# Dealing the sixteen row slots of a two-table expert gather from one pool instead of eight per table

## The chip, the cores and the metric

One Trainium2 chip, one core. The metric is the device time of one execution of the program, in microseconds (us). Names of the engines: PE is TensorE, DVE is VectorE, ACT is ScalarE, POOL is GpSimd, SP is SyncE.

## What is computed

A decoder trunk of two layers over 256 tokens of 1024 float32 features. Layer 0 is a short gated convolution and an expert network, layer 1 stick-breaking attention and an expert network of the same form; a final norm ends it. The expert network is what matters here:

```python
def one_chunk(xc):                                   # 128 tokens
    q = (xc @ w_query).reshape(C, HEADS, 2, KEY_DIM) # 8 heads
    ...
    idx = ...                                        # 16 experts of 16384 per token and head
    gate = softmax(top_s)
    act = gelu(einsum('chkd,cd->chk', u_tbl[idx], xc))
    coef = gate * act
    return einsum('chk,chkd->cd', coef, v_tbl[idx])
```

For each token, head and choice one row of 1024 floats is read from the table u and one from the table v. That is 2 layers x 2 chunks x 8 heads x 16 choices = 512 gathers from u and 512 from v; one gather fetches a row for each of 128 tokens, 512 KB.

## The kernel before, in words

The work on the experts runs in 32 steps (`STEPS`, one chunk and head each, number n), and a step has two groups g of eight choices. The text numbers the groups K = 2n + g, from 0 to 63, and calls the sixteen gathers of a group, in the order of their issue, u0 to u7 and v0 to v7.

**POOL** issues all gathers, one after the other, in one program order: `gather_group` (line 674) issues u0 to u7 of a group and then v0 to v7. Each goes to a slot of the tile `rows`, sixteen slots of 128 x 1024 floats. The first eight belong to u, the other eight to v (lines 464 and 465), so each gather takes the slot of the gather sixteen places before it, and waits until that row has been used: u_j for the dot product of u_j of the group before (`dot_done`), v0 to v6 for PE's use of the same row of the group before (`v_used`), v7 for DVE's (`v_added`). A group with g = 0 also waits for the indices of its step (`expert_ready`).

**DVE** multiplies each landed u row with the tokens and sums it (`dot_group`, line 1707), one instruction for a row. In the middle of the eight, after the fourth, stands `add_row` (line 1698), which adds v7 of the group before. Then come the coefficients (`coefficients`, lines 1723 and 1726). After the first group of a step DVE searches the 16 best experts of the next step (`find_experts`, lines 1646 to 1676), a chain of some 35 small instructions, many of which wait for an earlier one by a semaphore of DVE's own; only then does it take the dots of the second group. The text calls this chain the search.

**ACT** takes the gelu of the eight dots (line 1266) and makes a diagonal matrix from each coefficient (line 1274); **PE** multiplies the diagonal with the v row and accumulates over all choices (`combine`, line 897), v0 to v6 in order, and signals `v_used` after each. In the last group v0, v1, v2 and v4 and half of v7 go to PE (`combine_tail`, lines 909 and 916) and the others to DVE (line 1922).

**SP** streams the weights of the convolution and the attention in blocks of 1 MB through other buffers, while the gathers run. The gathers' issue order and the weights' order are both written out; no planner moves them. At the start the row slots also hold early weights, and slot 14 holds a gain (`first_gain`, line 467).

Arrivals are counted by one semaphore for each j: `u_landed[j]`, `v_landed[j]`, 16 per landing.

Of the kernel before, what the change touches and what calls it, by code (L numbers as in the profile page):

```python
# [26 lines left out]
ACT = mybir.ActivationFunctionType  # L27
# [11 lines left out]
U_SLOTS = 8  # L39
# [4 lines left out]
def trunk(nc, x, norm_mix, norm_ffn, conv_w_in, conv_kernel, conv_w_out, norm_kv, w_kv,  # L44
# [22 lines left out]
    PE_ROWS = GROUPS * BY_PE  # L67
    SLOTS = HEADS * GROUPS
    fills, FILL = [], {}
    turn = {"block": [0, 1], "side": [2, 3]}  # L70
# [319 lines left out]
    with ExitStack() as ctx:  # L390
# [76 lines left out]
        first_gain = v_row[6]  # L467
        w_place = [wring[:, j] for j in range(W_RING)] + [
# [156 lines left out]
        def _(pool):  # L625
# [25 lines left out]

            def gather(row, j, table, n, k, landed):

                nc.gpsimd.indirect_dma_start(  # L654
                    row[j], None, table,
                    bass.IndirectOffsetOnAxis(ap=expert[n % 2][:, k:k + 1], axis=0)).then_inc(landed[j], 16)

            def first_group():

                early_weights_used(0)  # L660
                pool.wait_ge(expert_ready, 1)
                for j in range(GROUP):
                    if j % 2 == 0 and j:
                        early_weights_used(j)
                    gather(u_row, j, u_table, 0, j, u_landed)
                for j in (6, 7, 0, 1, 2, 3, 4, 5):
                    if j == 6:
                        pool.wait_ge(first_near, 1)
                        pool.sem_inc(slot_clear, 1)
                    if j % 2 == 0:  # L670
                        early_weights_used(U_SLOTS + j)
                    gather(v_row, j, v_table, 0, j, v_landed)
# [18 lines left out]
            first_group()  # L691
            for K in range(1, GROUPS * STEPS):
                gather_group(K // GROUPS, K % GROUPS)
# [3 lines left out]
        def _(pe):  # L697
# [190 lines left out]
            def combine(n, b, g, end=TOPK):  # L888
# [4 lines left out]
                for k in range(g * GROUP, min(end, g * GROUP + BY_PE)):  # L893
                    pe.wait_ge(diag_ready, PE_ROWS * n + BY_PE * g + k % GROUP + 1)
                    pe.wait_ge(v_landed[k % V_SLOTS], 16 * (GROUPS * n + g + 1))
                    for half in range(2):
                        last = nc.tensor.matmul(sums[:, half, :], diag[:, k % GROUP, :],  # L897
                                                v_row[k % V_SLOTS][:, half * 512:(half + 1) * 512],
                                                start=(first and k == 0), stop=(k % GROUP == BY_PE - 1),
                                                skip_group_check=True)  # L900
                    last.then_inc(v_used, 1)

            def combine_tail(n):

                for i, k in enumerate(TAIL_PE):
                    pe.wait_ge(diag_ready, PE_ROWS * n + BY_PE + i + 1)
                    pe.wait_ge(v_landed[k % V_SLOTS], 16 * (GROUPS * n + 2))
                    for half in range(2):
                        last = nc.tensor.matmul(sums[:, half, :], diag[:, k % GROUP, :],
                                                v_row[k % V_SLOTS][:, half * 512:(half + 1) * 512],  # L910
                                                start=False, stop=(half == 0 and k == TAIL_PE[-1]), skip_group_check=True)
# [3 lines left out]
                pe.wait_ge(v_landed[k % V_SLOTS], 16 * (GROUPS * n + 2))  # L915
                nc.tensor.matmul(sums[:, 1, :], diag[:, k % GROUP, :], v_row[k % V_SLOTS][:, 512:D],
                                 start=False, stop=True, skip_group_check=True).then_inc(v_used, 1)
# [275 lines left out]
        def _(act):  # L1193
# [330 lines left out]
            for half in range(2):  # L1524
                cols = slice(half * D // 2, (half + 1) * D // 2)
                act.wait_ge(stream_ready, half + 1)
                nc.scalar.activation(u_row[0][:, cols], h[:, 1, cols], ACT.Square, accum_out=stat[:, 0, half:half + 1]).then_inc(squares, 1)
            act.wait_ge(means, normed_count("final", 1))
# [5 lines left out]
        def _(dve):  # L1534
# [157 lines left out]
            def add_row(n, b, g, chunk):  # L1692

                dve.wait_ge(v_landed[BY_PE], 16 * (GROUPS * n + g + 1))
# [3 lines left out]
                nc.vector.scalar_tensor_tensor(out=h[:, chunk, :], in0=v_row[BY_PE], scalar=coef[b][:, g * GROUP + BY_PE:(g + 1) * GROUP],  # L1698
                                               in1=h[:, chunk, :], op0=ALU.mult, op1=ALU.add).then_inc(v_added, 1)

            def dot_group(n, b, g, js=range(GROUP), late=None):
                for j in js:
                    k = g * GROUP + j
                    if late and j == GROUP // 2:
                        add_row(*late)
                    dve.wait_ge(u_landed[j], 16 * (GROUPS * n + g + 1))
                    nc.vector.scalar_tensor_tensor(out=u_row[j], in0=u_row[j], scalar=1.0,  # L1707
                                                   in1=xn_near[:, :, :].rearrange("p a d -> p (a d)"),
# [210 lines left out]
            for k, cols in [(k, slice(0, D)) for k in TAIL_DVE] + [(TOPK - 1, halves_of_d[0])]:  # L1919
                j = k % V_SLOTS  # L1920
                dve.wait_ge(v_landed[j], 16 * (GROUPS * last + 2))
                need(mark(nc.vector.scalar_tensor_tensor(out=h[:, 1, cols], in0=v_row[j][:, cols], scalar=coef[1][:, k:k + 1],
                                                         in1=h[:, 1, cols], op0=ALU.mult, op1=ALU.add)))
# [47 lines left out]
```

## Time and profile before

| | |
|---|---|
| median of 3 runs | 1693.29 us (1691.18 to 1697.15) |
| the profiled execution | 1688.29 us, its span 1686.3 us |
| busy: PE, DVE, POOL, ACT | 1325.6, 1052.9, 988.3, 366.5 us |
| moved by DMA | 607.66 MB, of which the gathers 536.94 MB; mean 360 GB/s |
| mean granted PE clock | 0.879 |

The profiled execution is 5.0 us below the median. All stretches are given in us from the start of its span. In a row of the timeline the columns are: start, duration, engine, line, operation, tiles, count, and in brackets the idle time of the engine before it with what ended that idle time. "issue" in that place means that nothing in the profile is seen to end it, "remote" that a semaphore arrived whose writer the profile does not tell. In a row of the windows view the columns are: stretch, its length, then busy us (and instructions) of PE, of PE's weight loads, of DVE, ACT and POOL, then the granted PE clock, the DMA engines' mean busy share, and GB/s.

### The profile page before, as it was taken

Reading aid. Unit: us, or ns where it says so; the run is one execution under the profiler, and the core shown is the slowest. Engines: PE = TensorE matmul, PEld = TensorE weight load, DVE = VectorE, ACT = ScalarE, POOL = GpSimd, SP = SyncE. Lnnn points to the kernel's source line nnn. Section 1 sums busy time; section 2 is a strip of 40 time slices with the busy share of each in tenths; the row PEclk is TensorE's granted clock in tenths of the full one; section 3 lists DMA queues with packets and bytes.
Section 4 is the critical chain, followed back from the end, with each engine's and each line's share of the span. In section 5 each row is a group of like instructions: output and inputs, shape, how many; then the busy total and the mean of one; then the engine's idle time right before and its main releaser. Section 6 shows DMA issues by size and latency. Waiting matters only on the chain.

```text
span 1686.3 us, 15100 instructions
## 1 busy us (share of the span) xinstructions
PE 1325.6 (79%) x4882; PEld 765.0 (45%) x4882; DVE 1052.9 (62%) x2495; ACT 366.5 (22%) x843; POOL 988.3 (59%) x1038
## 2 busy tenths in 40 slices
PE   9989788778768798849876899878987786665556
PEld 8976544344335454324543455535454442222222
DVE  3447477656766576655767845566667663866665
ACT  1111232112212223222212232133222221211101
POOL 0046466667666566646566765466666656666754
PEclk9989899889789898868898999889997988777778
DMA  9589999999999999999999999799999989899997
GB/s 333 178 302 339 359 340 358 375 391 382 381 368 355 342 401 406 399 408 404 385 404 378 360 400 404 293 397 328 373 406 365 349 299 385 323 365 368 377 334 301
DMA packets 197713, 607.66 MB, mean 360 GB/s; under 512 B 17597, under 2 KB 50437, under 8 KB 197637
## 3 DMA queue, kind: packets, MB, share of 16 engines
q0 software_dynamic: 147456, 536.94, 83.4%
q1 hardware_dynamic: 50048, 69.73, 11.9%
q8 instruction: 40, 0.66, 0.2%
q14 instruction: 37, 0.30, 0.1%
q10 hardware_dynamic: 132, 0.04, 0.0%
HBM read 605.59 MB, written 1.05 MB: 360 GB/s over the span
## 4 chain that ended last, share of the span: by engine, by line
PE 39%; DVE 16%; issue 14%; DMA 10%; POOL 10%; another core or an unknown queue 7%; ACT 3%; SPq 1%; POOLq 0%; DVEq 0%; ACTq 0%
PE sums L897 24%; POOL rows L654 10%; DVE rows L1707 8%; PE banks L754 8%; DMA rows<-in_peer_u,expert 6%; PE banks L771 4%; DMA rows<-in_peer_v,expert 3%; DVE h L1698 1%; DMA wring<-in_attn_w_q 1%; PE banks L780 1%; PE sums L763 1%; DMA h<-in_x 1%; DVE find L1606 1%; ACT soft_diag L1274 1%
## 5 line engine op out<-in xcount | busy, mean ns | idle before, releaser
L897 PE MATMUL sums<-rows,soft_diag 128*128 128x512 f32 x1764 | 865.4, 648 | 255.5 <-ACT soft_diag L1274 127.4
L654 POOL DMA_INDIRECT rows<-in_peer_v,expert x512 | 502.4, 981 | 448.8 <-PE sums L897 190.1
L1707 DVE SCALAR_TENSOR_TENSOR rows<-rows,xn_near 128x1024 f32<-128x1024 f32 x512 | 603.3, 1217 | 206.6 <-DMA rows<-in_peer_u,expert 176.6
L897 PEld LDWEIGHTS sums<-rows,soft_diag 128*128 128x128 f32 x1764 | 361.8, 209 | 727.7 <-issue 587.7
L654 POOL DMA_INDIRECT rows<-in_peer_u,expert x512 | 483.8, 945 | 235.8 <-issue 147.8
L1274 ACT ACTIVATE soft_diag<-ident,coef 128x128 f32<-128x128 f32 x446 | 138.4, 389 | 39.7 <-issue 22.6
L1266 ACT ACTIVATE gelu<-dots 128x8 f32<-128x8 f32 (+1 forms) x65 | 13.5, 208 | 582.7 <-DVE rows L1707 341.1
L1698 DVE SCALAR_TENSOR_TENSOR h<-rows,coef,h 128x1024 f32<-128x1024 f32 x63 | 80.7, 1281 | 0.0
L754 PE MATMUL banks<-xT,wring 128*128 128x128 f32 x512 | 65.0, 285 | 13.0 <-issue 10.6
L754 PEld LDWEIGHTS banks<-xT,wring 128*128 128x128 f32 x512 | 63.0, 201 | 18.0 <-issue 17.8
L1769 DVE SCALAR_TENSOR_TENSOR soft_diag<-banks,soft_diag 128x512 f32<-128x512 f32 (+1 forms) x8 | 7.7, 958 | 98.0 <-ACT soft_diag L1299 66.5
L1210 ACT ACTIVATE scores<-banks 128x256 f32<-128x256 f32 (+1 forms) x38 | 18.1, 478 | 169.9 <-PE banks L802 52.3
L754 PE MATMUL banks<-xT,rows 128*128 128x128 f32 x448 | 51.4, 276 | 1.8 <-issue 1.4
L1266 ACT ACT_TABLE_LOAD x41 | 52.6, 1283 | 0.7
L754 PEld LDWEIGHTS banks<-xT,rows 128*128 128x128 f32 x448 | 50.6, 192 | 2.5 <-issue 1.6
L771 PE MATMUL banks<-gain_ffnT,wring 128*128 128x128 f32 x256 | 38.3, 314 | 10.1 <-issue 8.6
L771 PEld LDWEIGHTS banks<-gain_ffnT,wring 128*128 128x128 f32 x256 | 36.6, 227 | 13.2 <-issue 11.2
L1707 DVE DVE_READ_ACCUMULATOR rows<-rows,xn_near 128x1 f32 x512 | 42.1, 82 | 0.0
L754 PE MATMUL banks<-xT,wkept 128*128 128x128 f32 x256 | 33.9, 285 | 9.6 <-issue 9.3
L1258 ACT ACT_TABLE_LOAD x31 | 39.8, 1283 | 0.5
L1663 DVE TENSOR_TENSOR find<-digit,iota 128x512 f32<-128x512 uint32 x31 | 21.5, 692 | 28.7 <-remote 16.0
L754 PEld LDWEIGHTS banks<-xT,wkept 128*128 128x128 f32 x256 | 32.1, 200 | 12.4 <-issue 12.0
(209 smaller groups left out, 1019.7 us busy)
## 6 DMA issues: line engine op xcount, KB each, us to landing
wring<-in_w_kv SPq DMA_DIRECT2D x14, 1024.0 KB
rows<-in_peer_u,expert POOLq DMA_INDIRECT x512
rows<-in_peer_v,expert POOLq DMA_INDIRECT x512
wkept<-in_peer_w_query SPq DMA_DIRECT2D x8, 1024.0 KB
rows<-in_conv_w_in SPq DMA_DIRECT2D x7, 1024.0 KB, 11.9
wring<-in_peer_w_query SPq DMA_DIRECT2D x7, 1024.0 KB
wring<-in_attn_w_q SPq DMA_DIRECT2D x7, 1024.0 KB
wkept<-in_conv_w_out SPq DMA_DIRECT2D x4, 1024.0 KB
```

Source lines behind the costliest of these rows:

```text
L654: nc.gpsimd.indirect_dma_start(row[j], None, table, bass.IndirectOffsetOnAxis(ap=expert[n % 2][:, k:k + 1], axis=0)).then_inc(landed[j], 16)
L754: last = nc.tensor.matmul(bank[:, s * tokens:(s + 1) * tokens], w[:, k, s * P:(s + 1) * P], xt[:, k, :], start=(k == 0), stop=(k == KT - 1))
L763: last = nc.tensor.matmul(bank, xt[:, k, :], w[:, k, :], start=(k == 0), stop=(k == KT - 1))
L771: last = nc.tensor.matmul(bank[:, s * P:(s + 1) * P], w[:, k, s * P:(s + 1) * P], xt[:, kh * KT // 2 + k, :], start=(kh == 0 and k == 0 an ...
L897: last = nc.tensor.matmul(sums[:, half, :], diag[:, k % GROUP, :], v_row[k % V_SLOTS][:, half * 512:(half + 1) * 512], start=(first and k ...
L1210: nc.scalar.activation(dst, view(banks[:, fills[n][1], :]), ACT.Copy, scale=scale).then_inc(bank_read["act"], 1)
L1258: nc.scalar.activation(gate[b][:], top[b][:], ACT.Exp, bias=negmax[:, b:b + 1], accum_out=gate_sum[:, b:b + 1]).then_inc(gate_done, 1)
L1266: nc.scalar.activation(gelu[b][:, ks], dots[b][:, ks], ACT.Gelu).then_inc(gelu_done, 1)
L1274: nc.scalar.activation(diag[:, j, :], ident[:], ACT.Copy, scale=coef[b][:, k:k + 1]).then_inc(diag_ready, 1)
L1663: d = mark(nc.vector.tensor_tensor(pick.rearrange("p a k j -> p (a k) j"), digit[:].rearrange("p a k -> p (a k)").unsqueeze(2).to_broadcas ...
L1698: nc.vector.scalar_tensor_tensor(out=h[:, chunk, :], in0=v_row[BY_PE], scalar=coef[b][:, g * GROUP + BY_PE:(g + 1) * GROUP], in1=h[:, chun ...
L1707: nc.vector.scalar_tensor_tensor(out=u_row[j], in0=u_row[j], scalar=1.0, in1=xn_near[:, :, :].rearrange("p a d -> p (a d)"), op0=ALU.mult, ...
```

## The change

A loop ahead of the program deals the slots: gather number i takes the slot whose `free_at` is smallest, and sets it to i plus a fixed life, 9 + 0.35 j gathers for u_j and 14.4 + 0.3 j for v_j. Each gather then waits for the use of whatever row held its slot before (`wait_slot_free`). Readers find the rows through the same table. The sixteen slots, the order of the gathers, and their number stay. `v_landed` becomes two semaphores per j, for even and odd groups, since a v row can now be asked for while the row with the same j of the group before has not been used up. The output square of the last norm (line 1527) goes to the slot of the last group's u7.

From group 2 on the table repeats with the group. The row that held the slot before, with the distance in gathers (K is the group's own number):

| gather | waits for the use of | | gather | waits for the use of |
|---|---|---|---|---|
| u0 | v5 of K-2, 19 back | | v0 | v0 of K-1, 16 back |
| u1 | u3 of K-1, 14 back | | v1 | v1 of K-1, 16 back |
| u2 | v6 of K-2, 20 back | | v2 | v2 of K-1, 16 back |
| u3 | u4 of K-1, 15 back | | v3 | u0 of K, 11 back |
| u4 | v7 of K-2, 21 back | | v4 | v3 of K-1, 17 back |
| u5 | u5 of K-1, 16 back | | v5 | u1 of K, 12 back |
| u6 | u6 of K-1, 16 back | | v6 | v4 of K-1, 18 back |
| u7 | u7 of K-1, 16 back | | v7 | u2 of K, 13 back |

In group 1, v2 takes u0 of its own group (10 back), v5 takes u1 and v7 takes u2; v0, v1 and all u keep 16.

```diff
+    ROWS = U_SLOTS + V_SLOTS
+    row_slot, row_before = [], []
+    holder, free_at = [None] * ROWS, [0] * ROWS
+    for i in range(STEPS * GROUPS * ROWS):
+        slot = i if i < ROWS else min(range(ROWS), key=lambda s: (free_at[s], s))
+        row_slot.append(slot)
+        row_before.append(holder[slot])
+        holder[slot] = i
+        free_at[slot] = i + (9 + 0.35 * (i % ROWS) if i % ROWS < U_SLOTS else 14.4 + 0.3 * (i % ROWS - U_SLOTS))
...
-        u_row = [rows[:, j, :] for j in range(U_SLOTS)]
-        v_row = [rows[:, U_SLOTS + j, :] for j in range(V_SLOTS)]
+
+        def u_row(K, j):
+            return rows[:, row_slot[ROWS * K + j], :]
+
+        def v_row(K, j):
+            return rows[:, row_slot[ROWS * K + U_SLOTS + j], :]
+
...
-        v_landed = [sem(f"v_landed{j}") for j in range(V_SLOTS)]
+        v_landed = [[sem(f"v_landed{j}_{odd}") for odd in range(2)] for j in range(V_SLOTS)]
...
+        def wait_v_landed(eng, K, j):
+            eng.wait_ge(v_landed[j][K % 2], 16 * (K // 2 + 1))
...
+            def wait_slot_free(i):
+
+                K, j = divmod(row_before[i], ROWS)
+                if j < U_SLOTS:
+                    pool.wait_ge(dot_done, GROUP * K + j + 1)
+                elif j < U_SLOTS + BY_PE:
+                    pool.wait_ge(v_used, BY_PE * K + j - U_SLOTS + 1)
+                else:
+                    pool.wait_ge(v_added, K + 1)
...
                 for j in range(GROUP):
-                    pool.wait_ge(dot_done, GROUP * (K - 1) + j + 1)
-                    gather(u_row, j, u_table, n, g * GROUP + j, u_landed)
+                    wait_slot_free(ROWS * K + j)
+                    gather(u_row(K, j), u_table, n, g * GROUP + j, u_landed[j])
                 for j in range(GROUP):
-                    if j < BY_PE:
-                        pool.wait_ge(v_used, BY_PE * (K - 1) + j + 1)
-                    else:
-                        pool.wait_ge(v_added, K)
-                    gather(v_row, j, v_table, n, g * GROUP + j, v_landed)
+                    wait_slot_free(ROWS * K + U_SLOTS + j)
+                    gather(v_row(K, j), v_table, n, g * GROUP + j, v_landed[j][K % 2])
...
-                    pe.wait_ge(v_landed[k % V_SLOTS], 16 * (GROUPS * n + g + 1))
+                    wait_v_landed(pe, GROUPS * n + g, k % V_SLOTS)
```

The other readers (`combine_tail`, `add_row`, `dot_group`, lines 1527 and 1922) change in the same way.

## Rows read from the trace of the kernel before

**Rows 1.** The page: its span, and what the DMA engines moved.

```profile
span 1686.3 us, 15100 instructions
...
DMA packets 197713, 607.66 MB, mean 360 GB/s; under 512 B 17597, under 2 KB 50437, under 8 KB 197637
```

**Rows 2.** The windows view of five stretches (columns as said above).

```profile
180.00:580.00 400.00, 319.01 (x1071) 176.29 (x1069) 266.07 (x630) 86.35 (x216) 255.32 (x262) 0.88 0.98 365
580.00:1060.00 480.00, 393.40 (x1408) 219.88 (x1407) 305.25 (x699) 120.44 (x256) 297.83 (x311) 0.90 1.02 394
1100.00:1410.00 310.00, 255.67 (x852) 138.35 (x850) 202.53 (x466) 74.80 (x160) 191.37 (x201) 0.89 0.95 361
1410.00:1686.00 276.00, 164.20 (x326) 69.40 (x326) 173.18 (x395) 46.03 (x122) 172.67 (x180) 0.78 0.92 350
...
678.00:702.00 24.00, 19.14 (x40) 8.62 (x40) 15.12 (x27) 7.05 (x14) 15.99 (x17) 0.79 1.03 409
```

**Rows 3.** Waits of POOL: waited for, us in total, times, longest us.

```profile
POOL rows L654 <- PE sums L897: 190.1, 119, 15.7
POOL rows L654 <- remote: 87.4, 35, 4.7
...
POOL rows L654 <- DVE h L1698: 46.1, 15, 6.4
```

**Rows 4.** Timeline of POOL: v4 of group 5, v6 of group 14, v6 of group 63.

```profile
244.04 1.77 POOL L654 DMA_INDIRECT rows<-in_peer_v,expert  x1 [1.40 <-PE sums L897]
...
457.02 0.94 POOL L654 DMA_INDIRECT rows<-in_peer_v,expert  x1 [3.65 <-remote]
...
1671.21 1.23 POOL L654 DMA_INDIRECT rows<-in_peer_v,expert  x1 [3.70 <-PE sums L909]
```

**Rows 5.** Timeline of POOL: v3 and v6 of group 50.

```profile
1357.20 0.94 POOL L654 DMA_INDIRECT rows<-in_peer_v,expert  x1 [0.78 <-PE sums L897]
...
1362.35 0.94 POOL L654 DMA_INDIRECT rows<-in_peer_v,expert  x1 [0.78 <-PE sums L897]
```

**Rows 6.** Timeline: v0 of group 10, PE's seven rows of group 57, v1 of group 58.

```profile
355.80 1.08 POOL L654 DMA_INDIRECT rows<-in_peer_v,expert  x1 [3.64 <-PE sums L897]
...
1528.93 13.84 PE L897 MATMUL sums<-rows,soft_diag 128*128 128x512 f32 x28 [10.04 <-ACT soft_diag L1274]
...
1547.47 0.94 POOL L654 DMA_INDIRECT rows<-in_peer_v,expert  x1 [4.25 <-remote]
```

**Rows 7.** Timeline of POOL: v3 and v7 of group 53, u0 of group 54.

```profile
1433.26 0.94 POOL L654 DMA_INDIRECT rows<-in_peer_v,expert  x1 [4.71 <-remote]
...
1442.44 0.93 POOL L654 DMA_INDIRECT rows<-in_peer_v,expert  x1 [4.51 <-DVE h L1698]
1443.68 0.94 POOL L654 DMA_INDIRECT rows<-in_peer_u,expert  x1 [0.30 <-issue]
```

**Rows 8.** Timeline of DVE: a step of a search, its last, the first dot of group 53.

```profile
1423.18 0.09 DVE L1611 MATCH_VALUE_LOAD side_i<-side_v,find 128x8 f32 x1 [3.90 <-remote]
...
1436.24 0.17 DVE L1676 TENSOR_SCALAR expert<-expert_f 128x16 uint32<-128x16 f32 x1
1436.33 1.21 DVE L1707 SCALAR_TENSOR_TENSOR rows<-rows,xn_near 128x1024 f32<-128x1024 f32 x1
```

**Rows 9.** The windows view, over two searches (DVE is the third busy number).

```profile
1412.20:1436.40 24.20, 13.87 (x28) 5.87 (x28) 8.66 (x36) 5.12 (x11) 14.45 (x16) 0.78 0.95 367
1504.50:1513.50 9.00, 8.44 (x16) 3.80 (x17) 8.48 (x35) 5.12 (x11) 6.86 (x7) 0.79 0.84 283
```

**Rows 10.** Timeline of POOL: u0 of groups 52, 60 and 62.

```profile
1394.56 0.94 POOL L654 DMA_INDIRECT rows<-in_peer_u,expert  x1 [0.31 <-issue]
...
1580.06 0.93 POOL L654 DMA_INDIRECT rows<-in_peer_u,expert  x1 [0.30 <-issue]
...
1628.81 0.94 POOL L654 DMA_INDIRECT rows<-in_peer_u,expert  x1 [0.30 <-issue]
```

**Rows 11.** The chain that ended last, near its end: start, us, what.

```profile
1672.74 5.09 DMA rows<-in_peer_v,expert
```

More of the change, by code:

```diff
@@ L650, in early_weights_used, with gather @@
                     pool.sem_inc(slot_clear, 1)
-            def gather(row, j, table, n, k, landed):
+            def gather(row, table, n, k, landed):
                 nc.gpsimd.indirect_dma_start(
-                    row[j], None, table,
-                    bass.IndirectOffsetOnAxis(ap=expert[n % 2][:, k:k + 1], axis=0)).then_inc(landed[j], 16)
+                    row, None, table,
+                    bass.IndirectOffsetOnAxis(ap=expert[n % 2][:, k:k + 1], axis=0)).then_inc(landed, 16)
+            def wait_slot_free(i):
[6 more added lines that the diff above has]
+                    pool.wait_ge(v_added, K + 1)
             def first_group():
@@ L664, in first_group @@
                         early_weights_used(j)
-                    gather(u_row, j, u_table, 0, j, u_landed)
+                    gather(u_row(0, j), u_table, 0, j, u_landed[j])
                 for j in (6, 7, 0, 1, 2, 3, 4, 5):
@@ L671, in first_group @@
                         early_weights_used(U_SLOTS + j)
-                    gather(v_row, j, v_table, 0, j, v_landed)
+                    gather(v_row(0, j), v_table, 0, j, v_landed[j][0])
             def gather_group(n, g):
@@ L681, in gather_group @@
                 for j in range(GROUP):
-                    pool.wait_ge(dot_done, GROUP * (K - 1) + j + 1)
-                    gather(u_row, j, u_table, n, g * GROUP + j, u_landed)
+                    wait_slot_free(ROWS * K + j)
+                    gather(u_row(K, j), u_table, n, g * GROUP + j, u_landed[j])
                 for j in range(GROUP):
-                    if j < BY_PE:
-                        pool.wait_ge(v_used, BY_PE * (K - 1) + j + 1)
-                    else:
-                        pool.wait_ge(v_added, K)
-                    gather(v_row, j, v_table, n, g * GROUP + j, v_landed)
+                    wait_slot_free(ROWS * K + U_SLOTS + j)
+                    gather(v_row(K, j), v_table, n, g * GROUP + j, v_landed[j][K % 2])
             first_group()
+            assert all(before is None or i - before < 2 * ROWS for i, before in enumerate(row_before))
             for K in range(1, GROUPS * STEPS):
@@ L1526, in _ @@
                 act.wait_ge(stream_ready, half + 1)
-                nc.scalar.activation(u_row[0][:, cols], h[:, 1, cols], ACT.Square, accum_out=stat[:, 0, half:half + 1]).then_inc(squares, 1)
+                nc.scalar.activation(u_row(GROUPS * STEPS - 1, U_SLOTS - 1)[:, cols], h[:, 1, cols], ACT.Square, accum_out=stat[:, 0, half:half + 1]).then_inc(squares, 1)
             act.wait_ge(means, normed_count("final", 1))
@@ L1692, in add_row @@
             def add_row(n, b, g, chunk):
[L1694 removed]
+                wait_v_landed(dve, GROUPS * n + g, BY_PE)
                 dve.wait_ge(coef_ready, GROUPS * n + g + 1)
@@ L1697, in add_row @@
                     dve.wait_ge(v_added, GROUPS * n + g)
-                nc.vector.scalar_tensor_tensor(out=h[:, chunk, :], in0=v_row[BY_PE], scalar=coef[b][:, g * GROUP + BY_PE:(g + 1) * GROUP],
+                nc.vector.scalar_tensor_tensor(out=h[:, chunk, :], in0=v_row(GROUPS * n + g, BY_PE), scalar=coef[b][:, g * GROUP + BY_PE:(g + 1) * GROUP],
                                                in1=h[:, chunk, :], op0=ALU.mult, op1=ALU.add).then_inc(v_added, 1)
@@ L1706, in dot_group @@
                     dve.wait_ge(u_landed[j], 16 * (GROUPS * n + g + 1))
-                    nc.vector.scalar_tensor_tensor(out=u_row[j], in0=u_row[j], scalar=1.0,
+                    nc.vector.scalar_tensor_tensor(out=u_row(GROUPS * n + g, j), in0=u_row(GROUPS * n + g, j), scalar=1.0,
                                                    in1=xn_near[:, :, :].rearrange("p a d -> p (a d)"),
@@ L1920, in _ @@
                 j = k % V_SLOTS
-                dve.wait_ge(v_landed[j], 16 * (GROUPS * last + 2))
-                need(mark(nc.vector.scalar_tensor_tensor(out=h[:, 1, cols], in0=v_row[j][:, cols], scalar=coef[1][:, k:k + 1],
+                wait_v_landed(dve, GROUPS * last + 1, j)
+                need(mark(nc.vector.scalar_tensor_tensor(out=h[:, 1, cols], in0=v_row(GROUPS * last + 1, j)[:, cols], scalar=coef[1][:, k:k + 1],
                                                          in1=h[:, 1, cols], op0=ALU.mult, op1=ALU.add)))
```

12 lines of the change are left out of this document (6 added, 6 removed).

## The prediction

> **What bounds the kernel now.** I read the page first, then the windows by stretch, then POOL's waits, then the timelines of single groups, and at last the chain that ended last. The kernel moves 607.66 MB [rows 1]. The fastest stretch shows 409 GB/s [rows 2]; at that rate all bytes would take 607.66 / 0.409 = 1486 us, against a span of 1686.3. So some 200 us pass with the DMA engines below their rate, though their busy share reads 0.9 to 1.0 nearly everywhere. By stretch: from 580 to 1060, where weights are streamed beside the gathers, 394 GB/s; in the three stretches without much of them 365, 361 and 350 [rows 2]. Only in those three can earlier gathers bring much.
>
> There POOL is what starves the DMA. Gathers that wait for nothing start 1.24 us apart (from 1442.44 to 1443.68 [rows 7]), so a group cannot take less than 19.8 us, and real ones take about 23. The rest is POOL's waits for slots. They sum to 190.1 + 87.4 + 46.1 us in 119 + 35 + 15 waits [rows 3]; without the 0.30 that every gather shows, that is 323.6 - 50.7 = 273 us. Most are one pause of 2 to 4 us per group.
>
> The pause isn't what it seems. PE has done the seven rows of group 57 by 1528.93 + 13.84 = 1542.8, yet v1 of group 58, which needs the second of them, waits until 1547.47 [rows 6]. PE's signal is late, and it arrives after POOL has been silent for some 4 us. DVE's search shows the same: the same 35 or 36 instructions, 8.5 to 8.7 us of work, took 9.0 us at 283 GB/s and 24.2 us at 367 [rows 9], with single gaps of 3.90 us between two small instructions [rows 8]. The long one followed group 52, in which POOL did not wait once. I read this as: the longer the gathers run without a pause, the later the engines' signals get.
>
> **The change, part by part.** POOL's instructions, their order and count stay, SP's queue is not touched, and a wait costs the same 0.30 whichever semaphore it reads; the added semaphores and the new addresses cost nothing that a row shows. What changes is which use each gather waits for, and the table of the change gives four cases.
>
> (1) v0, v1 and v2 keep their predecessor, 16 back. All waits that begin there stay: the 3.6 at v0 of group 10, the 4.25 at v1 of group 58 [rows 6]. By my reading of the timeline these are over half of the 273 us. Gain 0.
>
> (2) v7 waited for `add_row`. It now waits for the dot of u2, three instructions earlier, but v3 waits for the dot of u0. In group 53 that dot starts at 1436.33 and lasts 1.21 [rows 8], so v3 could go at 1437.54 + 0.30 = 1437.8 and v7 four gathers later, at 1442.8; it went at 1442.44 [rows 7]. The 46.1 us of waits for `add_row` [rows 3] are thus not won: the pause moves from v7 to v3, and v7 comes 0.4 us later. Nine groups outside the first stretch look so: +3.6 us. In the groups from 580 to 1060 v3 will come up to 8 us later, which the transfers queued there cover (409 GB/s with 15.99 of 24 us of POOL issuing [rows 2]); without that cover it would be 8 us a group.
>
> (3) v4 to v6 wait for a row one or two places earlier, and v5 and v6 of a group are needed only by u0 and u2 two groups on. Pauses that begin at v3 to v6 should go. Outside the DMA-bound stretch, and where the dot of u0 isn't late, I count twelve, from v4 of group 5 (1.40 - 0.30 = 1.1 us) over v6 of group 14 (3.35) to v6 of group 63 (3.4) [rows 4], together 24.8 us. The last is the surest: the landing of the last gather, 5.09 us from 1672.74, lies on the chain's end [rows 11].
>
> (4) Where PE was late with its first row, POOL follows it row by row, 0.78 - 0.30 = 0.48 us a gather [rows 5]. With v3, v5 and v7 bound to dots, up to four of these go, 1.8 us a group. In most such groups the next v0 waits for PE anyway and takes it back; in six it doesn't: 6 x 1.8 = 10.8 us.
>
> So 35.6 us of waits go. Against it stand (2) with 3.6, and group 1, whose v2 now waits for u0 of its own group: 1.7 us by moving that wait into its timeline.
>
> (5) What is late next: the signals. POOL ran through groups 52, 55 and 60 without any wait; after 52 and 60 the search took about 24 us, after 55 nothing happened. The two steps so begun lasted 1443.68 - 1394.56 = 49.1 and 1628.81 - 1580.06 = 48.8 us, the three between them (1580.06 - 1443.68) / 3 = 45.5 [rows 7, 10]. A group without a pause costs its step 3.5 us more. Eight of the groups in (3) have a search behind them. Two thirds of eight, times 3.5: 18.7 us given back. The bounds are 0 and 8 x 3.5 = 28.
>
> Sum: -35.6 + 3.6 + 1.7 + 18.7 = -11.6 us. On the profiled execution's 1688.29 that gives 1676.7; the median shown lies 5.0 above it, so 1682.
>
> The Trainium skill (DMA: Bandwidth & Descriptors, Specifications) gives about 358 GB/s as the HBM limit of one core; by it 607.66 MB would need 1697 us, the kernel would be at its limit, and the sum would be 0. The trace disagrees: 394 GB/s stood for 480 us [rows 2].
>
> **The rivals.** *No change, 0.25.* Every pause that goes comes back, at v0 to v2 of the next group or as a stretched search: 35.6 - 28 - 5.3 = 2.3 us are left, 1691. For it: the pause seems to be how the signals catch up [rows 6], and v0 to v2 are untouched. The DMA engines being at their rate already would give 1693 too; the 409 against 350 to 365 [rows 2] speak against that.
>
> *Slower, 0.30.* v3 asks for a dot of its own group. Eleven gathers at 1.24 are 13.6 us, so it decides whether the dot of u0 starts later than 13.6 - 1.2 = 12.4 us after u0's issue. When the search is stretched it does: u0 of group 53, sixteen gathers after 1394.56 + 19.8, went at 1414.4, its dot came 21.9 us later [rows 8, 10]. If fewer pauses early in a group make more searches long, more steps go as 52/53 did. Of the 20 steps outside the DMA-bound stretch two do so now; each more costs 3.5 us against the 30.3 won, so the point is nine more. With 13 more: +15 us, 1708; with all 18: 1726. For it: two of three groups without waits. Against it: most pauses begin at v0 to v2 and stay, and they reset the signals.
>
> *Larger gain, 0.08.* Nothing is given back: -30.3, 1663. For it: group 55. That the change doesn't do what it says I exclude: the table follows from the loop.
>
> **How the numbers follow.** A measurement of this kernel can tell about 0.3%, 5.1 us. The forecast, a gain of 5 to 22 us, has 0.37, its own range 1671 to 1688; with the larger gain faster has 0.45, within 0.3% has 0.25, slower 0.30. The range 1660 to 1712 leaves out half of the larger gain and the far third of the slower case.
>
> **What would show it.** Right: waits of POOL at v3 to v6 by PE (rows like [rows 4]) gone, the last gather about 3 us sooner after u0 of its group; waits at v0 to v2 about as before; the waits for `add_row` [rows 3] gone and waits for dots (L1707) in their place, of similar sum; more than two searches above 20 us. Forecast wrong: rates in the three stretches unchanged or lower (no change or slower), or above 380 GB/s (larger gain); waits for L1707 well above 46 us together with odd groups' first dots later than 12.4 us (slower).

## The result, and the profile after

The changed kernel took 1713.12 us (median of 10 executions, 1694.52 to 1723.02) against 1693.67 (10 executions, 1688.45 to 1703.48): ratio 1.0085, 95% interval 1.0052 to 1.0118. The ratio here and below is one of means, and leaves out executions more than 1.5% above the fastest of their kernel, here the 1723.02 alone. The changed kernel is slower by 0.85%, where 1682 was forecast. The direction is clear; that 1713 stands 1.1 us outside the range and not inside it is less than the scatter (a second measurement, e11 below, gave 1703.79, against 1688.38 for the kernel before).

The profiled execution took 1723.02 us, 10 above its median, so its excess over [rows 1] overstates the loss; where it matters, e11's profile, which lies at its kernel's median, is set beside it. The page: its span, the engines' busy time, and what was moved.

```profile
span 1721.1 us, 15100 instructions
...
PE 1318.4 (77%) x4882; PEld 766.2 (45%) x4882; DVE 1050.4 (61%) x2495; ACT 367.0 (21%) x843; POOL 997.0 (58%) x1038
...
DMA packets 197712, 607.66 MB, mean 353 GB/s; under 512 B 17596, under 2 KB 50436, under 8 KB 197636
```

The windows view of the changed kernel, the stretches and columns of [rows 2], and at last the fourth stretch to the end of the span:

```profile
180.00:580.00 400.00, 302.42 (x1055) 170.93 (x1055) 261.02 (x627) 86.51 (x217) 245.89 (x256) 0.87 0.95 360
580.00:1060.00 480.00, 378.26 (x1299) 205.56 (x1297) 299.17 (x696) 118.59 (x258) 292.52 (x301) 0.89 0.99 380
1100.00:1410.00 310.00, 245.85 (x878) 140.27 (x878) 195.14 (x455) 76.29 (x161) 185.23 (x191) 0.88 0.91 346
1410.00:1686.00 276.00, 176.77 (x385) 78.67 (x385) 180.89 (x428) 50.42 (x130) 184.06 (x188) 0.81 0.94 357
1410.00:1721.00 311.00, 198.62 (x426) 87.43 (x425) 200.54 (x462) 56.05 (x145) 197.93 (x202) 0.81 0.91 347
```

365, 394 and 361 GB/s became 360, 380 and 346: the first three stretches lost, among them, with 394 to 380, the one in which I had called the wait of v3 covered. The 357 of the fourth is no gain on 350: up to 1686 the kernel before has ended, the changed one has not, and from 1410 to its end it moved 347. The waits of POOL, to be read against [rows 3]:

```profile
POOL rows L673 <- PE sums L924: 227.2, 95, 15.4
POOL rows L673 <- DVE rows L1734: 94.7, 74, 9.5
...
POOL rows L673 <- remote: 49.0, 22, 3.8
```

The waits for `add_row` (46.1 us) are gone, those for dots are there, 94.7 instead of a similar 46. Those put down to PE rose from 190.1 to 227.2, but those put down to "remote" fell from 87.4 to 49.0: together they are 277.5 and 276.2. What changed is where in the group they stand. By place in the group, without the 0.30 of every gather: v3 to v7 fell from 135.5 to 70.4 us, v0 to v2 rose from 157.5 to 214.1, u0 and u2 from under 1 to 34. All waits together went from 296 to 321 us. Thirteen groups ran without a wait over 0.5 us, three did before. Fewer pauses, and more time. In e11 v0 to v2 rose by 31 us and the u rows by 17, and all waits together by only 4.

Waits aren't all. The gathers' own time on POOL rose too: mostly 0.94 us each, some take up to 2 us, and POOL was busy for 997.0 us (997.5 in e11) against 988.3 before. That is 9 us. Up to the end of the last gather, e11 is 13.4 us later than the kernel before: 4 by waits, 9 by longer gathers.

Where such a run leads is best seen in groups 49 to 51. POOL's timeline: the last two v of group 50, the first and last u of group 51, its v0.

```profile
1399.51 0.94 POOL L673 DMA_INDIRECT rows<-in_peer_v,expert  x1 [0.30 <-PE sums L924]
1400.76 0.94 POOL L673 DMA_INDIRECT rows<-in_peer_v,expert  x1 [0.30 <-issue]
1402.00 0.94 POOL L673 DMA_INDIRECT rows<-in_peer_u,expert  x1 [0.30 <-issue]
...
1410.69 0.94 POOL L673 DMA_INDIRECT rows<-in_peer_u,expert  x1 [0.30 <-issue]
1422.66 0.94 POOL L673 DMA_INDIRECT rows<-in_peer_v,expert  x1 [11.03 <-PE sums L924]
```

And PE's timeline in the same stretch (start, duration, count in a row, idle time before):

```profile
1399.24 2.62 PE L798 MATMUL banks<-gain_ffnT,wkept 128*128 128x128 f32 x22
1402.70 0.27 PE L798 MATMUL banks<-gain_ffnT,wkept 128*128 128x128 f32 x1 [0.84 <-issue]
1404.10 0.39 PE L798 MATMUL banks<-gain_ffnT,wkept 128*128 128x128 f32 x2 [1.13 <-issue]
...
1410.40 0.37 PE L798 MATMUL banks<-gain_ffnT,wkept 128*128 128x128 f32 x1 [1.73 <-issue]
1411.80 0.37 PE L798 MATMUL banks<-gain_ffnT,wkept 128*128 128x128 f32 x1 [1.02 <-issue]
1413.21 0.37 PE L798 MATMUL banks<-gain_ffnT,wkept 128*128 128x128 f32 x1 [1.04 <-issue]
1414.60 0.37 PE L798 MATMUL banks<-gain_ffnT,wkept 128*128 128x128 f32 x1 [1.02 <-issue]
1415.33 4.90 PE L798 MATMUL banks<-gain_ffnT,wkept 128*128 128x128 f32 x28 [0.35 <-issue]
```

This adds to the picture of the prediction. I had read "PE's signal is late". Here PE itself stands: the matmuls with the weights, for which the profile shows nothing that they wait for, come one or two at a time, some 1.4 us apart, and flow again 3.7 us after POOL's last gather has ended. It doesn't explain the case of [rows 6]: there PE's rows were done, by the profile's modelled end, and v1 of group 58 still went some 4 us after POOL's gather before it had ended. The windows of the same stretch:

```profile
1390.00:1402.00 12.00, 11.86 (x50) 7.04 (x49) 7.93 (x13) 0.00 (x0) 9.03 (x10) 1.00 1.01 402
1402.00:1412.00 10.00, 2.54 (x8) 1.77 (x7) 0.00 (x0) 0.00 (x0) 7.50 (x8) 0.64 1.02 408
1412.00:1422.00 10.00, 7.59 (x39) 6.53 (x39) 6.94 (x32) 4.92 (x13) 0.00 (x0) 0.67 0.39 156
```

For 10 us only POOL and the DMA engines get on, at 408 GB/s; PE has 8 matmuls, ACT waits for PE's bank and DVE for ACT. Then the row sums of group 50 are late (they stand behind the weights in PE's order), POOL waits 11 us, and the rate drops to 156. The same is seen on DVE, in the search after group 34, where small instructions stand 1.6 to 2.5 us apart and the search took 18.2 us:

```profile
974.21 0.09 DVE L1638 MATCH_VALUE_LOAD cand_i<-top,find 128x8 f32 x1 [2.37 <-remote]
976.30 0.15 DVE L1686 TENSOR_SCALAR negmax<-top 128x1 f32<-128x1 f32 x1 [1.59 <-remote]
979.10 0.69 DVE L1690 TENSOR_TENSOR find<-digit,iota 128x512 f32<-128x512 uint32 x1 [2.49 <-remote]
```

I call this the stutter. On PE it can be summed: idle time of PE ahead of its matmuls into `banks` that nothing visible ended was 70.8 us before and 99.0 us after. It is a measure of how often PE stands, not of time lost: where PE isn't what the others wait for, it costs nothing.

### The profile page after: what moved, and what is told of

It reads as the page before. It is cut to its first block, busy times and chain, and to the rows that moved or that the text cites. A ratio compares the mean times of both kernels' runs of the same rounds, so it can differ in the third digit from the quotient of the medians.

```text
span 1721.1 us, 15100 instructions
## 1 busy us (share of the span) xinstructions
PE 1318.4 (77%) x4882; PEld 766.2 (45%) x4882; DVE 1050.4 (61%) x2495; ACT 367.0 (21%) x843; POOL 997.0 (58%) x1038
## 4 chain that ended last, share of the span: by engine, by line
PE 41%; DVE 21%; issue 14%; another core or an unknown queue 8%; DMA 8%; POOL 5%; ACT 3%; DVEq 0%; ACTq 0%; POOLq 0%
PE sums L924 22%; DVE rows L1734 11%; PE banks L781 9%; DMA rows<-in_peer_u,expert 7%; POOL rows L673 5%; PE banks L798 3%; DVE h L1725 2%; DMA rows<-in_peer_v,expert 1%; PE banks L807 1%; ACT soft_diag L1301 1%; DVE find L1633 1%; PE banks L839 1%; PE sums L790 1%; DVE side_i L1638 1%
## 5 line engine op out<-in xcount | busy, mean ns | idle before, releaser
L924 PE MATMUL sums<-rows,soft_diag 128*128 128x512 f32 x1764 | 854.5, 643 | 269.5 <-issue 143.9
L673 POOL DMA_INDIRECT rows<-in_peer_v,expert x512 | 509.1, 994 | 440.2 <-PE sums L924 210.2
L781 PE MATMUL banks<-xT,wring 128*128 128x128 f32 x512 | 65.4, 286 | 14.4 <-issue 14.3
L1750 DVE RECIPROCAL gate_inv<-gate_sum 128x1 f32<-128x1 f32 x32 | 5.2, 163 | 73.5 <-ACT gelu L1293 43.0
L798 PE MATMUL banks<-xT,wring 128*128 128x128 f32 x256 | 36.1, 296 | 10.2 <-issue 9.8
```

What stands on the lines that cost most here:

```text
L673: nc.gpsimd.indirect_dma_start(row, None, table, bass.IndirectOffsetOnAxis(ap=expert[n % 2][:, k:k + 1], axis=0)).then_inc(landed, 16)
L781: last = nc.tensor.matmul(bank[:, s * tokens:(s + 1) * tokens], w[:, k, s * P:(s + 1) * P], xt[:, k, :], start=(k == 0), stop=(k == KT - 1))
L798: last = nc.tensor.matmul(bank[:, s * P:(s + 1) * P], w[:, k, s * P:(s + 1) * P], xt[:, kh * KT // 2 + k, :], start=(kh == 0 and k == 0 an ...
```

## The experiments

The kernels ran on several chips, of two kinds: on two of them (e1 to e4; e5 to e8) the kernel before takes 1555.5 us, on three (e9 to e11; e12 to e15; e16 to e18), as in the first measurement, 1688 to 1694. Each run was compared with the kernel before on its own chip, and the kinds are told of separately. Whether it is the chip itself or something else that used it at the time isn't on record.

### Where the kernel before takes 1555.5 us

The first eight runs. `FROM` is a table of distances that stands for the loop of the change; a place not in it is 16 back. `FIRST` holds the exceptions of group 1.

**e1 and e8**, the changed code with the old dealing:

```diff
-        slot = i if i < ROWS else min(range(ROWS), key=lambda s: (free_at[s], s))
...
+    FROM = {}
...
+        before = FIRST[p] if K == 1 and p in FIRST else i - FROM.get(p, ROWS)
```

> The changed kernel with the dealing alone undone: its table gives every gather the slot of the gather 16 before, as in the kernel before; two v_landed semaphores per row and all waits by table stay. All theories that blame the dealing (A: signals come late when POOL issues without a pause; B: v3 to v7 wait for dots of their own group) expect the time of before, 1694 us within 0.3% (1689 to 1699). C, that the added semaphores or the waits by table cost something, expects the changed kernel's 1713.

1555.25 against 1555.51 us, ratio 0.9996 (0.9987 to 1.0005); again 0.9998 (0.9989 to 1.0007).

**e2** frees v7 alone of `add_row`, **e3** and **e6** (a repeat) give v5, v6 and v7 to dots that lie 13 back, so that none is 10 to 12 back:

```diff
+    FROM = {15: 13, 4: 21, 3: 15, 2: 15}
...
+    FROM = {13: 13, 14: 13, 15: 13, 0: 19, 2: 20, 4: 21, 1: 14, 3: 15}
```

> A smaller exchange: v7 takes u2 of its own group (13 back), u4 takes v7 of two groups before (21 back), u2 and u3 take u3 and u4 of the group before (15 back), all others 16 back. The waits of v7 for add_row (46 us in before) go, v3 to v6 keep their PE rows. B (v3 bound to the dot of u0 costs) expects this at or below before, 1685 to 1694, since v3 is free of dots. A (late signals) expects it between before and after, 1694 to 1706, since one pause in six goes and the searches get slower for it.

> Three u slots of the own group still go to v, but later: v5, v6, v7 take u0, u1, u2 (13 back, where the changed kernel has 11, 12, 13); u0, u2, u4 take v5, v6, v7 of two groups before (19, 20, 21 back); u1 and u3 take u3 and u4 (14, 15 back); the rest 16 back, v3 and v4 with it. B expects most of the loss back: waits for dots (66 us at v3 in the changed kernel) fall by about 2.5 us in each of some 15 late groups, time 1690 to 1700. A expects it as slow as the changed kernel, 1706 to 1716, for the pauses at v5 to v7 still go.

0.9997 (0.9988 to 1.0006), 0.9999 (0.9990 to 1.0008), 0.9998 (0.9988 to 1.0007). No dealing of these moves the time.

**e4** puts a pause into every group of the changed kernel:

```diff
+                pool.wait_ge(u_landed[GROUP - 1], 16 * (K + 1))
                 for j in range(GROUP):
                     wait_slot_free(ROWS * K + U_SLOTS + j)
```

> The changed kernel with one wait more: ahead of v0 of each group POOL waits until u7 of the same group has landed, so all gathers in flight are drained once a group (about 4 us of silence, 63 times; where v0 already waited 3 us or more it costs little). A expects the searches at 9 to 11 us nearly everywhere, the waits at v3 shorter, and the time no worse than 1713, perhaps back at 1700. B and anything else that takes a pause for a pure loss expects 1713 plus about 1 to 4 us in the 35 groups that did not pause there: 1760 to 1830.

1819.95 us, 1.1699 (1.1673 to 1.1725): waiting for the eighth u row empties the DMA queue in each group, 456.3 us of waits in 63. It shows what an empty queue costs, nothing of the stutter, since this chip has none. The question that its expectation asked, whether a pause in every group would help, got no answer where the stutter is.

**e5**, the changed kernel itself:

> The changed kernel itself, once more, against before on one chip. The first experiments ran on a chip where before took 1555.5 us and not 1694, with every search at 9 us and the DMA at 404 GB/s. D: on such a chip the DMA is the bound, and the changed kernel takes the same 1555 us as before within 0.3%. A: on a chip where before takes about 1694 and searches reach 14 to 24 us, the changed kernel is again 0.5 to 1.2% slower.

1559.49 against 1555.78 us, 1.0022 (1.0013 to 1.0032), 3.7 us. **e7** fetches half of each row (512 floats, from group 2 on, so that the sums leave out the other half; the dots are scaled by 0.03):

> The slots of before, but from group 2 on each gather fetches 512 floats of a row and not 1024 (the other halves are left unread, so the output isn't the reference's; the dots are scaled by 0.03 to keep stale numbers small). POOL still issues as often; the DMA has half the bytes. If late signals come from the load on the DMA, no search is above 10 us on any chip, and POOL's pace of 1.24 us or PE and DVE bound the kernel: 1400 to 1480 us. If they come from POOL's issuing, searches of 14 to 24 us stay on a chip that shows them.

1455.79 us (one execution), at 236 GB/s: 100 us shorter with half of the gathered bytes. From u0 of group 18 to u0 of group 46 it took 597.6 us against e8's 678.6: there the bytes set the time. From group 46 to 62 it took 333.4 against 334.7, so there they do not; that is 20.8 us a group, close to the 19.8 of gathers 1.24 us apart, POOL's own pace. Its expectation set the load on the DMA engines against POOL's issuing as the cause of late signals. That stays open, since it never ran where there are any. The windows view of e8 (old dealing):

```profile
180.00:580.00 400.00, 334.10 (x1220) 187.67 (x1218) 278.05 (x651) 92.42 (x228) 275.31 (x283) 0.91 1.02 402
580.00:1060.00 480.00, 383.54 (x1378) 213.17 (x1379) 322.77 (x749) 129.29 (x275) 300.39 (x315) 0.89 1.03 403
1060.00:1410.00 350.00, 285.91 (x940) 150.21 (x938) 259.84 (x602) 84.26 (x194) 252.55 (x261) 0.91 1.02 406
```

402 to 406 GB/s for 1230 us, every search 8.9 to 9.4 us long, and 0.6 us of stutter, in the old dealing and in the new. The traces of the two kinds differ in the stutter and in a tail of slow packets (last section), and the kernel before is 133 to 138 us shorter on this one. That the stutter makes this difference is likely, not shown. POOL's waits and the engines' busy time in e8, and then in e5:

```profile
POOL rows L676 <- PE sums L927: 137.1, 203, 5.5
POOL rows L676 <- DVE h L1728: 84.3, 30, 10.9
...
PE 1278.9 (82%) x4882; PEld 739.9 (48%) x4882; DVE 1060.2 (68%) x2495; ACT 363.1 (23%) x843; POOL 988.4 (64%) x1038
```

```profile
POOL rows L673 <- DVE rows L1734: 147.6, 141, 8.6
...
POOL rows L673 <- PE sums L924: 54.5, 77, 3.9
...
PE 1278.2 (82%) x4882; PEld 741.3 (48%) x4882; DVE 1060.8 (68%) x2495; ACT 362.8 (23%) x843; POOL 1007.0 (65%) x1038
```

The change does what it says: by place in the group the waits beyond 0.30 sum to 143 us instead of 160. But POOL is busy for 1007.0 us instead of 988.4: what the waits lose, the gathers gain. The same holds for the others: e1 with 982.0 us, e2 with 997.2, e3 and e6 with 1004.6 and 1004.7 take the same time. Most of it is at v6, here in group 21 (the others around it take 0.94):

```profile
583.57 1.86 POOL L673 DMA_INDIRECT rows<-in_peer_v,expert  x1 [0.30 <-issue]
```

The 3.7 us are lost by group 6, whose u0 goes at 227.8 us against 224.0 in e8 and 225.2 in e1, and the distance to e8 is 2.6 us at group 62: that fits group 1's own exchange (v0 of group 2 already goes 2.1 us later), and not the waits of v3 in the other groups. No run on this chip took the two apart.

### Where the kernel before takes 1688 to 1694 us

Here the executions of one kernel scatter by some 8 us (standard deviation), and what the ratio leaves out cuts into that scatter. So the difference of the means of all executions stands beside it, with two standard errors; it is the better guide.

**e11** is the changed kernel again, **e9** and **e18** the changed dealing from group 2 on, **e10** that of group 1 alone (v2 takes u0 of its own group, 10 back; the first three gathers of group 2 are 19 back). The line of e9 and e18:

```diff
+        back = FROM.get(p, ROWS) if K >= 2 else ROWS
```

> The changed dealing from group 2 on; group 1 keeps 16 back. On a chip where the kernel before takes about 1555 us: if the 3.7 us of the full change come from group 1, where v2 waits for u0 of its own group 10 gathers back, this run stands at the kernel before (1555 to 1556.5). If they come from the later v3, which waits for u0 of its own group 11 back in 62 groups, it stays at 1559 to 1560. On a chip where the kernel before takes about 1694 us: group 1 is one group of 63 there, so this run comes out slower than before by some 14 us by the theory that v3's dots cost it, and about 10 us by the theory that group 1 has its own 4 us share.

> The changed dealing in group 1 alone (v2 takes u0 of its own group, 10 back), 16 back from group 2 on but for the first three gathers of group 2, which are 19 back. The opposite of the run before: 1559 to 1560 if group 1 is what costs, 1555 to 1556 if v3 is. On a chip where before takes about 1694 us: within 4 us of before either way.

> The changed kernel beside the two partial ones on the same chip. 1559 to 1560 where before takes 1555; on a chip where before takes 1694, 1700 to 1720, ratio near 1.0085.

> The changed dealing from group 2 on, group 1 16 back, a second time. On a chip at 1555: 1555 to 1556.5 if the 3.7 us of the full change come from group 1, 1559 to 1560 if from v3 in the other groups. On a chip at 1690: again 8 to 13 us slower than before, with u0 of group 6 at 247 to 249 us where the full change had 259; if the first result was chance, within 4 us of before.

**e12** changes the dealing from group 46 on, **e13** in groups 18 to 45, **e14** nowhere. The lines of e12, and the one of e13 that differs (`IN` holds the distances of the first new group):

```diff
+        back = ROWS
+        if 46 <= K < 99:
+            back = IN.get(p, FROM.get(p, ROWS)) if K == 46 else FROM.get(p, ROWS)
...
+        if 18 <= K < 46:
```

> The changed dealing from group 46 on, 16 back before. On a chip where the kernel before takes about 1690 us, by the theory that the loss is made in group 1 and where weights are streamed beside the gathers, and that the forecast's gain is real in the last stretch: 5 to 8 us faster than before (ratio 0.995 to 0.997), the stretch from group 50 to group 60 at 180 to 183 us against 185.5. By the rival that gathers without pauses make signals late everywhere: 2 to 4 us slower. On a chip where before takes about 1555 us: within 1 us of it.

> The changed dealing in groups 18 to 45 alone, 16 back elsewhere. At 1690 for the kernel before: by the first theory 10 to 20 us slower (ratio 1.006 to 1.012), groups 18 to 46 taking about 730 us instead of 710 to 715. By the rival of late signals everywhere, its share of 28 of 63 groups: 6 us slower. On a chip at 1555: the same within 1 us by the theory that group 1 costs the 3.7 there, 2 us slower by the theory of v3.

> Every gather 16 back, with the changed code. By both theories the same as before (ratio 0.997 to 1.003). If the changed code itself (the pairs of semaphores, the gain's and the output's slots) cost anything where signals are slow, it would be 5 us or more slower.

| changed dealing in | ratio (interval) | means, us | stutter, us | u0 of groups 6, 18, 46, 62 at, us |
|---|---|---|---|---|
| none (before) | | | 70.8 | 250.6, 528.9, 1244.4, 1628.8 |
| none (e14) | 0.9955 (0.9911 to 0.9999) | +1.8 ± 6.8 | 77.6 | 247.8, 522.8, 1250.8, 1631.2 |
| all (first) | 1.0085 (1.0052 to 1.0118) | +15.8 ± 5.5 | 99.0 | 258.2, 539.8, 1277.5, 1662.6 |
| all (e11) | 1.0091 (1.0058 to 1.0124) | +12.8 ± 4.6 | 95.1 | 259.3, 539.1, 1270.3, 1642.7 |
| group 1 (e10) | 1.0053 (1.0021 to 1.0084) | +6.0 ± 5.5 | 77.4 | 254.7, 530.8, 1239.2, 1620.7 |
| from 2 on (e9) | 1.0097 (1.0063 to 1.0130) | +11.9 ± 5.1 | 106.9 | 247.8, 531.1, 1250.1, 1631.5 |
| from 2 on (e18) | 1.0043 (1.0006 to 1.0080) | +6.2 ± 5.6 | 87.1 | 244.8, 524.0, 1252.2, 1626.9 |
| 18 to 45 (e13) | 1.0017 (0.9979 to 1.0055) | +8.7 ± 6.3 | 78.3 | 248.8, 527.3, 1244.3, 1628.1 |
| from 46 on (e12) | 0.9951 (0.9915 to 0.9988) | -4.8 ± 5.5 | 89.8 | 248.6, 527.8, 1255.3, 1634.5 |

The last two columns are of one profiled execution each, and these lie between 17 us below their kernel's median (e10) and 10 above (the first). Up to group 6 it is plain all the same: with group 1 changed, 254.7 to 259.3 us; without, 244.8 to 250.6. Averaged over the kernels that have the old or the new dealing in a stretch, the new one costs 9.3 us up to group 6, 3.6 from there to 18, 6.8 from 18 to 46 (719.9 to 726.7, in a scatter of 708 to 738), and gives 4.0 back from 46 to 62: 15.7 us, against the measured 12.8 and 15.8. Only the first of the four stands well clear of the scatter; the second does by a hair (279.2 to 283.3 us against 275.0 to 279.1). The two parts by whole runs, 6.0 for group 1 and 9 for the rest, each with an error of 5 to 6, add up to the same. POOL's busy time is 983.2 to 988.8 us where all or most groups have the old dealing (before, e14, e12) and 994.3 to 1001.8 with the new one in groups 18 to 45 or more (the first, e11, e9, e18, e13); e10, with 994.9, doesn't fit that, so a part of the 9 us can be scatter. The ratio of e12 lies below 1, but so does that of e14, where nothing is dealt anew. No kernel here beats the one before by more than the scatter.

How group 1's exchange costs 10 us shows in its timelines. e14 first, POOL at v2 and v7, then the changed kernel, POOL at v2, v7 and the next u0:

```profile
128.16 0.94 POOL L676 DMA_INDIRECT rows<-in_peer_v,expert  x1 [0.78 <-PE sums L927]
...
138.32 0.94 POOL L676 DMA_INDIRECT rows<-in_peer_v,expert  x1 [2.36 <-DVE h L1728]
```

```profile
134.56 0.94 POOL L673 DMA_INDIRECT rows<-in_peer_v,expert  x1 [6.30 <-DVE rows L1734]
...
141.27 0.94 POOL L673 DMA_INDIRECT rows<-in_peer_v,expert  x1 [0.30 <-DVE rows L1734]
142.52 0.94 POOL L673 DMA_INDIRECT rows<-in_peer_u,expert  x1 [0.30 <-issue]
```

POOL is 3 us later, as one would add up. But now it has issued eight gathers unbroken by the middle of PE's 32 matmuls with weights. PE in e14, then in the changed kernel:

```profile
141.73 3.74 PE L784 MATMUL banks<-xT,gain_ffnT 128*128 128x128 f32 x32
```

```profile
142.60 2.51 PE L781 MATMUL banks<-xT,gain_ffnT 128*128 128x128 f32 x21
145.94 0.38 PE L781 MATMUL banks<-xT,gain_ffnT 128*128 128x128 f32 x2 [0.82 <-issue]
147.35 0.51 PE L781 MATMUL banks<-xT,gain_ffnT 128*128 128x128 f32 x3 [1.03 <-issue]
148.08 0.27 PE L781 MATMUL banks<-xT,gain_ffnT 128*128 128x128 f32 x1 [0.22 <-issue]
149.50 1.08 PE L781 MATMUL banks<-xT,gain_ffnT 128*128 128x128 f32 x3 [1.15 <-issue]
151.61 0.59 PE L781 MATMUL banks<-xT,gain_ffnT 128*128 128x128 f32 x2 [1.03 <-issue]
153.73 8.80 PE L924 MATMUL sums<-rows,soft_diag 128*128 128x512 f32 x14 [1.54 <-issue]
```

The row sums of group 1 begin at 153.73 instead of 145.31, and v0 of group 2 goes at 157.6 instead of 151.5. The same 8 us later start shows in e10 (153.1) and e11 (154.9), and not in the kernels that leave group 1 alone (145.0 to 147.0). The way from 6 us there to 10 at group 6 is one stretched search more, in group 5: v3 then waits 6.7 us for the dot of its own group's u0.

**e15 to e17** ask what the stutter hangs on. With the old dealing, gather i also waits for the landing of gather i - 4 (then 5, 6):

```diff
+                K, j = divmod(i - 4, ROWS)
+                if j < U_SLOTS:
+                    pool.wait_ge(u_landed[j], 16 * (K + 1))
+                else:
+                    pool.wait_ge(v_landed[j - U_SLOTS][K % 2], 16 * (K // 2 + 1))
```

> 16 back, and before gather i POOL also waits for the landing of gather i - 4, so that no more than four gathers are under way. On a chip at 1690: if the late signals come from a deep queue of gathers, every search is near 9 us and the kernel gains 15 us or more; if they come from the DMA engines being busy whatever the depth, searches stay as they are; and where four gathers don't cover the latency, it loses 30 us or more. On a chip at 1555, where nothing is late: 5 to 30 us slower.

> 16 back, at most five gathers under way. On a chip at 1690 for the kernel before: four under way gave searches of 9.0 us throughout and 340 to 351 GB/s, 1800 us. If late signals come with a deep queue, searches stay at 9 us here and the rate rises by up to a quarter, so the kernel reaches 1650 to 1720. If they come with the DMA engines at their rate, searches above 12 us come back as soon as the rate passes some 365 GB/s, and the time lies between 1700 and 1750. On a chip at 1555: 1600 to 1680, searches 9.0.

> 16 back, at most six under way; before, up to 13 were in the stretch with the weights and five outside it, so the limit binds there and in bursts. On a chip at 1690: by the theory of the deep queue searches below 10 us in the stretch with the weights and a gain of 10 us or more; by the theory of the rate the searches stay long and the time is 1690 to 1710. On a chip at 1555, where the mean depth was 6 to 7: 5 to 40 us slower.

Four under way: 1799.73 us, ratio 1.0638 (1.0597 to 1.0678), 339 and 351 GB/s in the first two stretches, searches of 8.9 to 9.4 us throughout, stutter 2.2 us. Five: 1704.02, 1.0051 (1.0011 to 1.0091), 374 and 383 GB/s, five searches of 16.7 to 23.3 us, stutter 57.0; its profiled execution, 1677.60, was its fastest. Six: 1707.42, 1.0116 (1.0076 to 1.0156), seven of 16 to 25, stutter 103.6. POOL's waits in e15, and how PE's matmuls with the weights then run (groups of instructions; busy, mean ns, idle before), e15 and then the changed kernel:

```profile
POOL rows L676 <- DMA rows<-in_peer_v,expert: 289.9, 373, 4.2
POOL rows L676 <- DMA rows<-in_peer_u,expert: 267.2, 387, 3.2
```

```profile
L789 PE MATMUL banks<-xT,wring 128*128 128x128 f32 x512 | 59.4, 275 | 0.0
```

```profile
L781 PE MATMUL banks<-xT,wring 128*128 128x128 f32 x512 | 65.4, 286 | 14.4 <-issue 14.3
```

So the stutter goes when POOL pauses for a landing nearly each time (760 waits of 1008 gathers) and is back with one or two gathers more under way. Depth, rate and the length of POOL's unbroken runs all rise together between e15 and e16, so these runs don't say which of the three counts. On the other kind of chip none of them does it alone: there six gathers stood ahead of a new one on average in groups 2 to 17, against 3.4 here, the rate was 402 to 406 GB/s, and 26 groups of e5 ran without a wait, with no stutter at all. Nor does the profile show what PE stands for. The transfers of instructions look the same on both kinds: 40 of 16 KB, of 1.07 us in the median before and 1.08 in e8.

## Why the prediction was wrong

The forecast was a gain of 11.6 us, the result a loss of 13 to 16. Three terms failed: the waits of v0 to v2 put at nothing, group 1 at 1.7 us, and the gathers' own time, which had no term at all.

*What bounds the kernel*: right in that the DMA engines have time to spare while POOL pauses, and in the reading that long unbroken runs of gathers go with others being late; too weak in putting a price on that. That the pauses are mostly what is left after the other engines have stood still fits the groups shown; it wasn't measured for all.

*Step (1), v0 to v2 as before, 0*: this failed most. Their waits rose by 57 us, and in e11 by 31; there that and 17 us at u rows ate what v4 to v6 had won. A pause taken out at v3 to v6 lets POOL reach the next v0 sooner, and what v0 waits for comes no sooner. Step (4) says as much of "most such groups" and leaves them out of its sum, yet step (3) counts its twelve pauses in full.

*POOL's own time, no term*: "POOL's instructions, their order and count stay" is true, but their length didn't: 9 us more here, 19 on the other kind, where it takes back all that the waits lost.

*Step (2), +3.6*: the waits moved from v7 to v3 as worked out, but the cover that I named for the groups from 580 to 1060 is doubtful. In groups 18 to 38 the gathers that stand ahead of a new one fell from 6.0 on average to 4.5, and that stretch ran at 380 instead of 394 GB/s; averages and e13 put groups 18 to 45 at +7 to +9 us, with an error as large.

*Steps (3) and (4), -35.6*: the waits at v4 to v7 went from 114.6 us to 4.0 (27 in e11), as said, and by group 46 to 62 perhaps 4 us of it show in the time. The last wait of all was not won: v6 of group 63 waits for nothing, but u2 of that group waits 3.2 us, and the last gather goes 22.4 us after u0 of its group, as before.

*Group 1, +1.7*: mis-sized. It is 6 us alone and some 10 up to group 6 with the new dealing behind it: POOL is 3 us late, and PE's work with the weights then falls behind eight unbroken gathers. This is the clearest single piece of the loss, about half of it.

*Step (5), +18.7*: the sign was right, the place not. Searches summed to nearly the same excess as before (112 against 108 us beyond 9.0 each, in 31 searches). Much came back as the stutter of PE ahead of the row sums, so at v0. Had the other steps come as forecast (-30.3), the give-back and group 1's excess together would be 43 to 46 us for the measured +12.8 to +15.8, beyond my bound of 28, which counted searches alone.

*The rivals*: Slower was the right side with the wrong price. It wanted nine more steps like 52/53, with a stretched search ahead of v3's dot; only one more search of 18 us or more came (four against three). Its mechanism does show, in group 5 and in v3's waits of 6 to 9 us in groups 29, 33 and 49. "Larger gain" rested on group 55, one case.

## What to carry to other kernels

A pause of the issuing engine may be the time in which the others catch up: before removing it, look at what they do while it runs unbroken, also at instructions that wait for nothing. Of waits in one in-order queue, look for the one that is released last in a cycle: here the others were paid again there. Watch the length of the issuing instructions too, not only their waits. And a special case at the start of a table (one group, 10 back where the rest has 11 or more) can cost as much as all the rest: here 6 us of some 15.

## What the runs showed of the hardware

- Two kinds of chip for one program: 1555.5 us (53 executions within 3.4 us) and 1688 to 1694 (29 executions over 31 us), at a mean granted clock of 0.905 and 0.88. On the first no engine stutters (0.6 us). Of the gathers' 4 KB packets, 2.4% take over 250 ns on the second kind and 0.4% on the first; the median is 159 and 164 ns. Why is open.
- One core moved 402 to 406 GB/s for 1230 us (e8), and its shortest stretches on the other kind reach 408. The Trainium skill (DMA: Bandwidth & Descriptors, Specifications) gives about 358 GB/s per core as the HBM limit, and further down (Bandwidth) says that this is what each gets with both cores of the HBM domain streaming. This program runs on one core, so the traces don't contradict the page; they show that 358 wasn't this kernel's limit.
- On the second kind, while POOL issued gathers without a break and the DMA engines ran at 408 GB/s, PE advanced one or two instructions in about 1.4 us, until 3.7 us after POOL had stopped (changed kernel, 1402 to 1415), and DVE's small ones stood 1.6 to 2.5 us apart (974 to 979). On the first kind this is not seen.
- Issuing a gather takes 0.94 us mostly and up to 2.0 at times; with fewer pauses POOL's busy time rises (988.3 to 997.0 us, 988.4 to 1007.0).
- With at most four gathers under way (2 MB) the DMA engines moved 337 to 351 GB/s in the four stretches (e15), with five 374 and 383 in the first two (e16).
